# The last pair of experts kept on chip in a routed mixture of experts (f32, one core)

## What is computed

```python
x_new = x + gt1 * (jnp.concatenate([attn_x, ret_x], axis=-1) @ w_out[l])
h2 = _modulate(_rmsnorm(x_new, norm2_g[l]), sh2, sc2)
...
weights = p_g * (p_e / jnp.sum(p_e, axis=-1, keepdims=True))     # two experts of one group per token
...
def expert_block(args):
    x_blk, e = args
    return (jax.nn.silu(x_blk @ w_gate[e]) * (x_blk @ w_up[e])) @ w_down[e]
...
x_new = x_new + gt2 * y          # y: the two experts' rows, each times its weight
return _rmsnorm(x, final_norm_g)
```

## Time and profile before

| | us |
|---|---|
| median of 3 runs | 1687.97 (1687.83 to 1690.42) |
| the profiled execution | 1688.73 |
| its span, first to last instruction | 1687.0 |
| TensorE busy in it | 1563.1 |
| VectorE, ScalarE, GpSimd busy | 905.6, 520.5, 156.2 |
| granted TensorE clock, mean | 0.979 of full speed |
| DMA moved | 353.08 MB |

### The profile page before, as it was taken

How to read it: one execution, slowest core, us unless ns; L and a number is a source line. 1 busy time by engine, 2 the same in 40 slices (tenths; PEclk the granted TensorE clock), 3 DMA queues, 4 the chain that set the end, 5 groups by cost and what they waited for, 6 DMA issues and landing times.

```text
span 1687.0 us, 22747 instructions
## 1 busy us (share of the span) xinstructions
PE 1563.1 (93%) x8480; PEld 1077.8 (64%) x8480; DVE 905.6 (54%) x1571; ACT 520.5 (31%) x836; POOL 156.2 (9%) x203
## 2 busy tenths in 40 slices
PE   5999999799899989999999989999999898898985
PEld 2788888577788868788788877785343333332441
DVE  2876526666558645576788788876212112121124
ACT  4422221567243354454432476322000000000011
POOL 2000010033110100001302130210000000000003
PEclk9999999789999999999999999999999999999998
DMA  9243352101332311223343202349999999999995
GB/s 383 113 160 140 113 216 109 57 14 31 113 138 104 119 53 51 100 88 151 142 149 129 101 26 77 132 189 371 405 423 423 423 422 423 423 422 423 422 383 214
DMA packets 57620, 353.08 MB, mean 209 GB/s; under 512 B 7376, under 2 KB 7632, under 8 KB 20544
## 3 DMA queue, kind: packets, MB, share of 16 engines
q1 hardware_dynamic: 43200, 307.41, 45.5%
q0 software_dynamic: 9248, 35.63, 5.7%
q10 hardware_dynamic: 5088, 8.92, 1.4%
HBM read 332.53 MB, written 23.59 MB: 211 GB/s over the span
## 4 chain that ended last, share of the span: by engine, by line
PE 64%; DMA 14%; DVE 9%; ACT 5%; SPq 4%; issue 4%; POOL 1%; ACTq 0%; DVEq 0%; POOLq 0%
PE ps L2266 11%; PE ps L2268 11%; PE ps L2267 11%; DMA early<-in_experts 10%; PE ps L2821 7%; PE ps L2307 4%; PE ps L2841 4%; SPq L705 3%; PE ps L2779 3%; PE ps L2484 3%; PE ps L2508 2%; DMA early<-in_ada 2%; PE ps L2218 1%; PE ps L2501 1%; ACT p L994 1%
## 5 line engine op out<-in xcount | busy, mean ns | idle before, releaser
L2266 PE MATMUL ps<-whi,xth 128*128 128x512 f32 (+1 forms) x768 | 300.8, 392 | 2.6 <-DVE xtl L1728 1.7
L2268 PE MATMUL ps<-whi,xtl 128*128 128x512 f32 (+1 forms) x768 | 297.0, 387 | 0.0
L2267 PE MATMUL ps<-wlo,xth 128*128 128x512 f32 (+1 forms) x768 | 296.7, 386 | 0.0
L2821 PE MATMUL ps<-early,xe_t 128*64 128x512 f32 x904 | 207.6, 598 | 31.0 <-DMA early<-in_experts 25.2
L2821 PEld LDWEIGHTS ps<-early,xe_t 128*64 128x64 f32 x904 | 60.9, 136 | 171.7 <-issue 104.5
L2266 PEld LDWEIGHTS ps<-whi,xth 128*128 128x128 f32 x768 | 145.2, 189 | 33.5 <-DVE xtl L1728 3.4
L2268 PEld LDWEIGHTS ps<-whi,xtl 128*128 128x128 f32 x768 | 145.0, 189 | 29.5
L2267 PEld LDWEIGHTS ps<-wlo,xth 128*128 128x128 f32 x768 | 145.3, 189 | 27.8
L2100 DVE TENSOR_TENSOR hid<-hid,ps 128x256 f32<-128x256 f32 x33 | 13.9, 421 | 251.3 <-ACT hid L1280 251.3
L1336 DVE TENSOR_TENSOR wlo<-raw,whi 128x2048 fp32r<-128x2048 f32 (+3 forms) x52 | 103.2, 1984 | 62.9 <-ACT whi L911 62.1
L1280 ACT ACTIVATE hid<-ps 128x256 f32<-128x256 f32 x33 | 12.7, 385 | 391.7 <-PE ps L2821 391.7
(11 more groups left out here) (463 smaller groups left out, 2712.1 us busy)
## 6 DMA issues: line engine op xcount, KB each, us to landing
early<-in_experts SPq DMA_DIRECT2D x128, 1024.0 KB, 26.4
raw<-in_experts SPq DMA_DIRECT2D x51, 1024.0 KB, 25.1
raw<-in_ada SPq DMA_DIRECT2D x40, 1024.0 KB, 6.7
ring<-in_experts SPq DMA_DIRECT2D x15, 1024.0 KB, 27.7
raw<-in_even SPq DMA_DIRECT2D x14, 1024.0 KB, 5.7
raw<-in_second SPq DMA_DIRECT2D x10, 1024.0 KB, 5.0
early<-in_ada SPq DMA_DIRECT2D x8, 1024.0 KB, 18.3
pair_dram<-tmp ACTq DMA_DIRECT2D x60, 128.0 KB, 6.9
```

The source lines that it names most:

```text
L2266: nc.tensor.matmul(v, a[0], b[0], start=first, stop=False)
L2267: nc.tensor.matmul(v, a[0], b[1], start=False, stop=False)
L2268: return nc.tensor.matmul(v, a[1], b[0], start=False, stop=last)
L2821: mm = nc.tensor.matmul(ps[SLOT * t:SLOT * t + SLOT, 4 + s, :], xe_t[:, 2 * i + k, SLOT * s:SLOT * s + SLOT], w[:, D * k + 512 * t:D * k + ...
```

## The change

Experts 30 and 31 become the last pair and neither is stored. The overflow blocks (at least one is always run) come right after the 15 pairs, in TensorE's loop; `pair_dram` is gathered once the last of them is stored. Their first turn gathers the rows of experts 30 and 31 together. Expert 30's weights go to `ring[6..11]`, expert 31's to `ring[0..5]`, its pieces 2 to 5 only when `s_pair[2]` has reached 48, that is when the gathers of tiles 0, 1 and 2 have landed. A fifth piece of expert 28 is loaded ahead (`more[4]`, first of all on SyncE's queue for the experts), for which the scratch of dynamic DMA descriptors is made smaller. VectorE adds both gathered choices to the rows (`early`); TensorE puts the rows into PSUM by the identity (`rows_so_far`) and adds the rows of expert 30 and 31 (`late`) there, all but the last half tile of expert 30's before expert 31's pieces 2 and 3; ScalarE squares and VectorE scales straight from PSUM. The one-hots of the late rows are 128 wide, their transposes become 16 matmuls.

```diff
...
-MORE = 4
+GATES = 20
+MORE = 5
...
+            sp.dma_start(more[4][:], src["experts"][SINGLE - 2, 4]).then_inc(s_more, 16)
             filled(sp, "sout", "o", NT - 1)
...
             for i in range(PARTS):
                 sp.wait_ge(s_used, PARTS * (SINGLE - 4 if i < MORE else SINGLE - 2) + i + 1)
-                sp.dma_start(ring[i], src["experts"][SINGLE, i]).then_inc(s_ew[i], 16)
...
+                sp.dma_start(ring[i], expert(e, i)).then_inc(s_ew[i], 16)
+            for i in range(PARTS):
+                sp.wait_ge(s_used, PARTS * (SINGLE - 1) + i + 1)
+                sp.dma_start(ring[PARTS + i], src["experts"][EXPERTS - 2, i]).then_inc(s_ew[PARTS + i], 16)
...
                 for i in range(PARTS):
                     sp.wait_ge(s_used, PARTS * o + PARTS * (SINGLE - 1) + i + 1)
+                    if i == 2:
+                        sp.wait_ge(s_pair[2], rows_first)
                     sp.dma_start(ring[i], expert(e, i)).then_inc(s_ew[i], 16)
...
+            pool.dma_start(spare[P * 8:P * 8 + SLOT, :], src["x"][0][0:SLOT, :]).then_inc(s_pair[2], 16)
...
-            pool.wait_ge(s_zin, 32 * over + (32 + 16 * NT))
-            pool.wait_ge(s_used, PARTS * over + PARTS * (SINGLE + 1) + 2)
+            pool.wait_ge(s_zin, 32 * over + 16 * NT)
+            pool.wait_ge(s_used, PARTS * over + PARTS * SINGLE)
...
             for m in range(LT):
-                act.wait_ge(s_x4, m + 1)
-                own(nc.scalar.activation(wide_junk, h_rows[:, CT + m, :], ACT.Square, accum_out=ss[:, CT + m:CT + m + 1]), s_sq)
+                act.wait_ge(s_tr, over + (EXPERTS + 1 + m))
+                own(nc.scalar.activation(wide_junk, whole(m), ACT.Square, accum_out=ss[:, CT + m:CT + m + 1]), s_sq)
...
+            gates = tmp[:, 1, 64:64 + nb]
+            own(nc.vector.tensor_scalar(gates, col[:, 0:nb], extra, 32.0, ALU.is_equal, ALU.mult))
+            own(nc.vector.tensor_scalar(gates, gates, 16.0, None, ALU.add))
+            own(nc.vector.tensor_copy(blocks_i[:, GATES:GATES + nb], gates))
+            own(nc.vector.tensor_copy(blocks_i[:, 40:41], extra), s_blocks)
+            turns = window_first[:, PAIRS:WINDOWS]
...
+            def early(m):
                 x = h_rows[:, CT + m, :]
...
+                dve.wait_ge(s_pair[m], 48 if m == 2 else 32)
+                for c in range(2):
+                    own(nc.vector.scalar_tensor_tensor(x, pairs[:, m, c, :], early_w[:, 4 * c + m:4 * c + m + 1], x,
+                                                       ALU.mult, ALU.add), s_x4 if c else None)
...
+            hidden(over + SINGLE, 0)
+            hidden_turned(over + SINGLE, 0)
+            out_rows(over + SINGLE, 0, s_zin, 32 * over + 16 * NT, 8)
+            for m in range(LT):
+                early(m)
+            dve.wait_ge(s_silu, over + EXPERTS)
...
+            last = single_piece(over)
+            pe.wait_ge(s_chosen, 2)
+            v = begin("late")
+            for s in range(2):
+                for m in range(LT):
+                    for t in range(2):
+                        mm = nc.tensor.matmul(v[halves[t], SEQ * s + P * m:SEQ * s + P * m + P],
+                                              late_rows[:, m, halves[s]], ident[:], start=True, stop=True)
+            end(mm, "late")
+            in_product(over + PAIRS, 0, last_but_one)
+            in_product(over + PAIRS, 1, last, range(0, 2))
+            turn_hidden(over + SINGLE, 0)
+            out_product(over + SINGLE, 0, last_but_one)
...
             for m in range(LT):
...
+                sides = (0, 1) if m < LT - 1 else (0,)
+                rows_so_far(m, sides)
+                late(m, 0, sides)
+            in_product(over + PAIRS, 1, last, range(2, 4))
+            turn_hidden(over + (SINGLE + 1), 1, 5)
+            out_product(over + (SINGLE + 1), 1, last, 5)
+            pe.wait_ge(s_yev, over + (EXPERTS + 1))
+            for m in range(LT):
+                if m == LT - 1:
+                    rows_so_far(m, (1,))
+                    late(m, 0, (1,))
+                late(m, 1).then_inc(s_tr, 1)
...
-    nc = _bacc.Bacc("TRN2", target_bir_lowering=False, num_devices=1)
+    nc = _bacc.Bacc("TRN2", target_bir_lowering=False, num_devices=1, dynamic_dma_scratch_size=4096)
```

More of the change, by code:

```diff
@@ L2072, in _ @@
             one_hot(0)
-            nb = BLOCKS - EXPERTS
+            extra = route[:, 24:25]
+            own(nc.vector.tensor_scalar(extra, first[:, 32:33], 1.0, None, ALU.max))
+            nb = EXTRAS + 1
             at_b = tmp[:, 1, 48:48 + nb]
@@ L2144, in _ @@
                 out_rows(2 * q + 1, 1, s_yst[1], 32 * q + 16)
-            def single(o, nxt):
+            dve.wait_ge(s_yst[0], 32 * PAIRS + 16)
+            with dve.Fori(0, over) as o:
                 hidden(o + SINGLE, 0)
@@ L2186, in _ @@
[L2186 to L2189, removed]
+                own.free(nc.vector.scalar_tensor_tensor(h_rows[:, CT + m, :], whole(m), rstd[:, CT + m:CT + m + 1], final_g[:],
+                                                        ALU.mult, ALU.mult), s_fin)
+            hidden(over + SINGLE, 0)
[3 more added lines that the diff above has]
+                early(m)
@@ L2812, in single_piece, with in_product @@
                 return landed
-            def in_product(g, s, landed):
+            def in_product(g, s, landed, steps=range(4)):
                 pe.wait_ge(s_xt, 2 * g + 2)
-                for i in range(4):
+                for i in steps:
                     w = landed(s, i)
@@ L2870, in _ @@
             pair(PAIRS - 1, last_pair)
-            pe.wait_ge(s_chosen, 2)
-            turn(("late",), [late_rows[:, m, :] for m in range(LT)], [P * m for m in range(LT)])
-            evacuated(pe, "late")
-            def single(o, nxt):
+            with pe.Fori(0, over) as o:
                 landed = single_piece(o)
                 in_product(o + PAIRS, 0, landed)
-                if nxt:
-                    gather(o + PAIRS + 1, 0)
+                gather(o + PAIRS + 1, 0)
                 turn_hidden(o + SINGLE, 0)
-                if nxt:
-                    gather(o + PAIRS + 1, 1)
+                gather(o + PAIRS + 1, 1)
@@ L2883, in single @@
                 out_product(o + SINGLE, 0, landed)
[L2884 to L2903 removed]
+                turn_rows(o + PAIRS + 1, 0)
@@ new lines, in _, with rows_so_far @@
+            end(mm, "late")
[3 more added lines that the diff above has]
+            out_product(over + SINGLE, 0, last_but_one)
+            pe.wait_ge(s_yev, over + (SINGLE + 2))
+            evacuated(pe, "late")
+            def rows_so_far(m, sides=(0, 1)):
+                pe.wait_ge(s_x4, m + 1)
+                for t in sides:
+                    nc.tensor.matmul(ps[:, LAST_BANK[m] + t, :], ident[:], h_rows[:, CT + m, 512 * t:512 * t + 512],
+                                     start=True, stop=False)
```

179 lines of the change are left out of this document (81 added, 98 removed).

## The result

The changed kernel takes 1679.8 us in the median (six runs, 1678.8 to 1686.1) against 1688.8, a ratio of 0.995 with a 95% interval of 0.9934 to 0.9967: faster by 9 us, where 2.9 were forecast and the range ended at 1681.0. Timed twice more, it gave 1680.2 and 1681.2, with ratios of 0.9949 and 0.9952.

What follows compares the result with a forecast made beforehand. Weights bound nearly all of the mixture until 1559.69 us, then TensorE and its hand-overs; the chain summed to 1683.1 or 1684.7 against 1687.0, weighted -2.9, so 1687.97 became 1685.1 us, range 1681.0 to 1690.0.

Steps and rivals of the forecast that it cites:

- the part on the end: Behind expert 31's result: 15.7 us to the span's end where 27.1 passed before, -11.4, its last 6.35 us unchanged.
- the descriptor scratch: Smaller room for GpSimd's DMA descriptors: priced at nothing, between 0 and 1.2 us of added waits between gathers.
- the late matmuls: TensorE's 16 matmuls of 64 columns for the late rows: 1.1 to 3.2 us, taken as 2.9.
- the wait for the late rows: TensorE's 2.58 us wait before the first single block goes; with the transposes moved, the overflow block starts 3.2 us earlier.
- the earlier gathers: Behind the overflow block's store: first gather at 1633.4 to 1634.9 against 1655.13, 20 us earlier.
- the rows ahead of expert 31: Rows into PSUM on TensorE before expert 31's pieces 2 and 3: 10.8 us, 1.6 more if the clock falls (0.65).
- the last stage: From expert 31's result: 5.9 us adding its rows on TensorE, then 2.15 square to scaling and 1.29 scaling.
- VectorE's small operations: Six more ahead of the first pair's copy of rows: 1.3 us in all, covered by 2.64 us of idle time.
- Rival 1: Faster: rows at 2.65 us per tile, late rows 1.7 instead of 2.9, no clock fall; 1681.8 median, chance 0.22.
- Rival 2: Slower: clock at its lower level from the rows through expert 31's out-product, 1696.3, or 1690 with half; chance 0.08.
- Rival 3: Slower: the gate on expert 31's pieces 2 to 5 opens late and holds the block up, 1688 to 1690; chance 0.06.
- Rival 4: No gain: 1 us more at each of three new hand-overs (late copy, rows, fourth tile), 1688; chance 0.14.

## Why the prediction was wrong, point by point

**What bounds the kernel** held: the weights up to the last pairs, then TensorE and its hand-overs. The order in which the steps follow, and seven of the nine lines of the table above, held as well, one of them with the luck told there; they stand on rows 3 to 13.

**The step that failed** is in the part on the end: "from its end at 1680.65 to the end of the span 6.35, unchanged", together with the descriptor scratch "at nothing, between 0 and 1.2 us". I had looked at the scratch only as room for descriptors, where it could cost a wait, and took the 6.35 us as a constant of the program's end without asking what filled them. The last output had landed at 1684.3; the 2.7 us behind that had no owner in my sum. The term of 6.35 measured 3.05, a gain of 3.3 us: 2.4 are the drain, as the kernel before with only the smaller scratch shows (6.35 to 4.0), and 0.9 are the last output that lands sooner, whose cause stays open. With it the same sum gives 1681.8, and with the late matmuls as measured 1680.7, where the three medians are 1679.8 to 1681.2. The bounds of the scratch's term excluded a gain for no reason that a row gave. That is also why the range missed.

**Mis-sized:** the late matmuls, 1.8 us instead of 2.9. They were like the eight of the earlier trace rows in shape, and the granted clock was 1.00 in both places; why those took nearly twice as long each isn't shown. The lower bound of 1.1 was nearer than the 2.9.

**Right in size:** the wait for the late rows (2.6, by the kernel that undoes it alone), the earlier gathers (24.2), the rows ahead of expert 31 (12.65 with the clock's fall; in four of the six executions with this idle time of 3.5 us it fell, for a chance of 0.65), the last stage (9.3 from result to VectorE's end against 9.35), and the gate, which cost nothing and saves 4.2 to 5.4 us in the traces. Its worth I hadn't worked out.

VectorE's small operations at the start were covered, though the sign that I had named against it, a shift of the first pair, is there in the first profile: its first product starts at 1171.92 us, before at 1168.16. But in all fourteen traces VectorE's copy ahead of it begins 0.64 to 0.72 us behind the start of the transposes that it reads, so it waits for TensorE, and its own operations hold it up by 0.08 us at most. The first product starts between 1164.3 and 1170.1 in the other nine traces with the new tail: the sign scatters by more than the effect.

**The rivals.** Rival 1 had the right side and nearly the number, 1681.8, but by other steps: the rows did take 2.97 a tile, and only its half on the late matmuls was true. Rival 2: the clock fell once, for one tile, and was back: 0.58 and 0.57 in the windows above, 1.00 in the next. Behind the shorter waits that follow in the same stretch, 0.52 to 0.94 us, it stayed at 1.00. Rival 3 is out by the traces with and without the gate. Rival 4, three lost hand-overs, is out by the table. The rule of the Trainium skill that DMA engines take turns between queues, "DMA: Bandwidth & Descriptors", section "Queues, rings and completion order", agrees with the kernel without the gate: beside 4 MB of weights the gathers' landing went from at most 6.4 us to 13.6 (medians of eight). With the gate its 0.3 us can't be told from 0, as TensorE never waited for the fourth tile.

**What stays open.** From the last product of the pairs to the end the traces have 79.8 and 79.9 us before and 72.7 to 73.8 after, a gain of 6.7 in the mean; the medians have 8.4 to 9.0, with intervals that reach from 5.2 to 11. Whether the medians gain some 2 us ahead of that point is not settled. The last product starts at 1607.2, 1607.4, 1605.9 and 1604.3 us in the four traces of kernels with the old tail, and between 1603.1 and 1610.5 in the ten with the new one, which share nearly every instruction up to the mixture of experts (one more store of spare rows); the means are 1606.2 and 1606.0. The traces thus give no sign of a gain there, and the scatter would hide one of 2 us. They do show where the scatter comes from: the first pair's product already starts anywhere between 1164.0 and 1171.9. From there to the last product of the pairs it takes 438.9 to 440.2 us with the old tail and 438.4 to 439.8 with the new one, 0.6 less in the mean. So the traces show no more than 0.6 us gained within the pairs, and most of the scatter arises ahead of the first pair.

## What to carry to other kernels

Give every stretch of the end an owner, also the one behind the last output: look for the instruction that ends the program, drains included, before calling a stretch unchanged. Read a tail from a point where the work is the same in both kernels, not from zero, when the stretch ahead scatters by more than the gain, and read it in more than one execution: a wait that stands in only one of them can hide a term that was priced wrong. A range for an edit whose effect no row shows has to be open on both sides.

## What the runs showed of the hardware that I had not expected

GpSimd's drain at the program's end takes 7.9 to 8.0 us with the default descriptor scratch, 4.6 with 8 KB and 2.9 to 3.0 with 4 KB, in all fourteen traces, whatever the kernel did with its DMAs. And the start of the same work, 1600 us into the program, lay anywhere in 7.4 us among builds that hardly differ ahead of it: the kernel with the half tile moved had a tail some 3 us shorter and a median that didn't show it. An idle time of TensorE that changed nothing in the order of work still cost 1.65 us behind it: in executions of the same length of idle time (3.5 us) the granted clock fell in four and not in two.
